# Four raw-weight slots with their own places in the load order, and an earlier copy-out, in a Strassen-like down-projection

## What is computed

```python
def swiglu(h, w_gate, w_up, w_down):
    return (jax.nn.silu(h @ w_gate) * (h @ w_up)) @ w_down
...
    yp = yp + swiglu(rms_norm(yp, g_ffn[l]), w_gate[l], w_up[l], w_down[l])
    ys = ys + swiglu(rms_norm(ys, g_ffn[l]), w_gate[l], w_up[l], w_down[l])
y_prompt = rms_norm(yp, g_final)
y_sample = rms_norm(ys, g_final)
```

## Time and profile before

| | |
|---|---|
| median of 3 runs | 1066.26 us (1065.92 to 1066.47) |
| the profiled execution, its time | 1065.66 us |
| the profiled execution, its span | 1063.9 us |
| PE busy | 1022.2 us, 96% of the span |
| DVE, ACT, POOL busy | 59%, 37%, 36% |
| mean granted clock of PE | 0.99 of full speed |

### The profile page before, as it was taken

The page is one execution under the profiler, slowest core; times in us unless marked ns, Lnnn a source line. Parts: engine busy times, 40 slices in busy tenths (PEclk is TensorE's granted clock), DMA queues, the critical chain, the costliest instruction groups (busy, mean ns, idle before and its releaser), DMA issues.

```text
span 1063.9 us, 19541 instructions
## 1 busy us (share of the span) xinstructions
PE 1022.2 (96%) x7160; PEld 934.2 (88%) x7160; DVE 625.9 (59%) x943; ACT 391.0 (37%) x763; POOL 385.3 (36%) x445
## 2 busy tenths in 40 slices
PE   5999999999999699999999999999999969999996
PEld 5999998888887599999999999999999737877785
DVE  5376547665444766666676576567665554454524
ACT  5412144444232433333333333333334354424331
POOL 2010100000000437676686596686762300120045
PEclk9999999999999899999999999999999989999999
DMA  8211331101222434364454544643637898777714
GB/s 282 90 39 42 81 83 43 40 1 64 95 100 90 116 97 147 109 198 133 124 173 123 159 140 125 186 144 110 188 117 261 271 359 293 240 267 254 269 40 163
DMA packets 176258, 155.84 MB, mean 146 GB/s; under 512 B 22352, under 2 KB 143760, under 8 KB 176208
## 3 DMA queue, kind: packets, MB, share of 16 engines
q1 hardware_dynamic: 176208, 155.16, 46.1%
HBM read 114.17 MB, written 41.06 MB: 146 GB/s over the span
## 4 chain that ended last, share of the span: by engine, by line
PE 88%; DVE 4%; DMA 4%; POOL 1%; issue 1%; ACT 1%; SPq 0%; POOLq 0%; ACTq 0%; DVEq 0%
PE ps L1033 27%; PE ps L1034 26%; PE ps L1035 26%; DMA xd_in<-act_scratch 2%; PE ps L1070 1%; PE ps L1364 1%; PE ps L1205 1%; PE ps L1183 1%; DMA act_scratch<-act_sums 1%; DMA out_state_gmlp_v_sample<-work 1%; PE ps L1167 1%; DVE work L1831 1%; DMA y_acc_odd<-in_w_down 1%; DVE ln_st L1825 1%; DMA gain<-in_g_mix 0%
## 5 line engine op out<-in xcount | busy, mean ns | idle before, releaser
L1033 PE MATMUL ps<-x_forms,w_forms 128*128 128x256 f32 (+1 forms) x1232 | 354.0, 287 | 10.5 <-DVE w_forms L1746 8.3
L1034 PE MATMUL ps<-x_forms,w_forms 128*128 128x256 f32 (+1 forms) x1232 | 355.0, 288 | 0.0
L1035 PE MATMUL ps<-x_forms,w_forms 128*128 128x256 f32 (+1 forms) x1232 | 353.6, 287 | 0.0
L1033 PEld LDWEIGHTS ps<-x_forms,w_forms 128*128 128x128 f32 x1232 | 236.3, 192 | 11.2 <-DVE w_forms L1746 5.8
L1035 PEld LDWEIGHTS ps<-x_forms,w_forms 128*128 128x128 f32 x1232 | 236.1, 192 | 0.0
L1034 PEld LDWEIGHTS ps<-x_forms,w_forms 128*128 128x128 f32 x1232 | 235.8, 191 | 0.0
L1033 PE MATMUL ps<-w_dn,x_dn 128*128 128x512 f32 x308 | 121.3, 394 | 0.0
L1035 PE MATMUL ps<-w_dn,x_dn 128*128 128x512 f32 x308 | 119.9, 389 | 0.0
L1034 PE MATMUL ps<-w_dn,x_dn 128*128 128x512 f32 x308 | 119.9, 389 | 0.0
L1746 DVE TENSOR_TENSOR w_forms<-w_sums,w_forms 128x512 fp32r<-128x512 f32 x88 | 74.1, 843 | 68.1 <-ACT w_forms L1570 67.7
L885 POOL TENSOR_SCALAR meansq<-sumsq 128x1 f32<-128x1 f32 (+1 forms) x27 | 10.4, 386 | 256.3 <-ACT xn_ffn L1410 227.0
(11 more groups left out here) (234 smaller groups left out, 2071.2 us busy)
## 6 DMA issues: line engine op xcount, KB each, us to landing
xd_in<-act_scratch SPq DMA_DIRECT2D x35, 512.0 KB, 7.1
t_raw<-in_w_down SPq DMA_DIRECT2D x88, 128.0 KB, 2.6
act_scratch<-act_sums SPq DMA_DIRECT2D x22, 512.0 KB, 4.0
y_acc_odd<-in_w_down SPq DMA_DIRECT2D x22, 512.0 KB, 5.6
wd_in<-t_scratch SPq DMA_DIRECT2D x20, 512.0 KB, 7.1
wd_in<-in_w_down SPq DMA_DIRECT2D x15, 512.0 KB, 6.2
stage<-in_w_in SPq DMA_DIRECT2D x28, 256.0 KB, 3.6
w_stage_even<-in_w_gate SPq DMA_DIRECT2D x22, 256.0 KB, 3.4
```

Of the source, the lines that this page charges most:

```text
L1033: mm(out, wh, xh, start=first, stop=False, skip_group_check=onto)
L1034: mm(out, wh, xl, start=False, stop=False, skip_group_check=onto)
L1035: return mm(out, wl, xh, start=False, stop=last, skip_group_check=onto)
```

## The change

The raw loads of the sample's first half get four slots (each a whole row of `y_acc_odd`), those of the second half keep two; the places of the raw loads in SP's order are listed in a table of their own, RAW_LOADS, which names the group (n, g) before whose loads they stand; r2 and r3 go behind the loads of group 7, before `store_sums`. The turn after (1,0) is dropped and one after (1,4) added. And `copy_out(0)` stands on ScalarE behind the forming of two groups of stage 1 (k = 6 and 7), not six.

```diff
-SAMPLE_TURNS = {(0, 3): 2, (0, 5): 2, (1, 0): 2, (1, 1): 2, (1, 2): 2, (1, 3): 1,
+SAMPLE_TURNS = {(0, 3): 2, (0, 5): 2, (1, 1): 2, (1, 2): 2, (1, 3): 2, (1, 4): 1,
                 (3, 0): 2, (3, 2): 2, (3, 4): 2, (4, 0): 2, (4, 2): 2, (4, 3): 1}
-RAW_SLOTS = 2
+EARLY_SLOTS, LATE_SLOTS = 4, 2
+
+RAW_LOADS = {(1, 2): range(4, 6), (1, 5): range(6, 8), (2, 2): range(8, 10), (2, 4): range(10, 11),
+             (3, 5): range(11, 13), (4, 1): range(13, 15), (4, 3): range(15, 17), (5, 0): range(17, 19),
+             (5, 2): range(19, 21), (5, 4): range(21, 22)}
+
+def raw_slot(r):
+    return (r % EARLY_SLOTS, r // EARLY_SLOTS + 1) if r < CHUNKS else (
+        EARLY_SLOTS + (r - CHUNKS) % LATE_SLOTS, (r - CHUNKS) // LATE_SLOTS + 1)
...
-        raw = [y_odd[:, 2 * x:2 * x + 2, 0:512] for x in range(RAW_SLOTS)]
+        raw = [y_odd[:, x, :].rearrange("p (e c) -> p e c", e=2) for x in range(EARLY_SLOTS)]
+        raw += [y_odd[:, 2 * x:2 * x + 2, 0:512] for x in range(LATE_SLOTS)]
...
             def load_raw(r):
 
                 h, c = divmod(r, CHUNKS)
-                if r >= RAW_SLOTS:
-                    sp.wait_ge(raw_used, r - RAW_SLOTS + 1)
+                slot = raw_slot(r)[0]
+                if r < EARLY_SLOTS:
+                    sp.wait_ge(product_done, product_count(last, P4, 0))
+                elif r < CHUNKS:
+                    sp.wait_ge(raw_used, r - EARLY_SLOTS + 1)
                 else:
-                    sp.wait_ge(product_done, product_count(last, P4, 0))
+                    sp.wait_ge(raw_used, max(CHUNKS, r - LATE_SLOTS + 1))
...
-            for r in range(RAW_SLOTS):
+            for r in range(2):
                 load_raw(r)
             store_step(CHUNKS - 1, 1)
...
             for k in (GROUPS_A_FORM, GROUPS_A_FORM + 1):
                 load_w(k)
                 load_x(k)
+            for r in range(2, EARLY_SLOTS):
+                load_raw(r)
             store_sums(CHUNKS - 1)
...
                 for g in range(2 if n == 1 else 0, GROUPS_A_FORM):
-                    if g >= 2:
-                        for r in range(max(RAW_SLOTS, raws_before(n - 1, g - 2)), raws_before(n - 1, g - 1)):
-                            load_raw(r)
+                    for r in RAW_LOADS.get((n, g), ()):
+                        load_raw(r)
                     load_w(GROUPS_A_FORM * n + g)
                     load_x(GROUPS_A_FORM * n + g)
-                for r in range(raws_before(n - 1, 4), raws_before(n, 0)):
-                    load_raw(r)
...
             for n in range(STAGES - 1):
-                for g in range(GROUPS_A_FORM):
+                ahead = 2 if n == 0 else GROUPS_A_FORM
+                for g in range(ahead):
                     form_hi(n + 1, g)
                 if n in (0, 1, 3):
                     for t in range(TILES):
                         copy_out(n, t)
+                for g in range(ahead, GROUPS_A_FORM):
+                    form_hi(n + 1, g)
```

More of the change, by code:

```diff
@@ L477, in build @@
         sample_landed = [sem(f"sample_landed{x}") for x in range(2)]
-        raw_landed = [sem(f"raw_landed{x}") for x in range(RAW_SLOTS)]
+        raw_landed = [sem(f"raw_landed{x}") for x in range(EARLY_SLOTS + LATE_SLOTS)]
         raw_used = sem("raw_used")
@@ L801, in load_raw @@
                 h, c = divmod(r, CHUNKS)
-                if r >= RAW_SLOTS:
-                    sp.wait_ge(raw_used, r - RAW_SLOTS + 1)
-                else:
-                    sp.wait_ge(product_done, product_count(last, P4, 0))
-                sp.dma_start(raw[r % RAW_SLOTS], w_down[:, 2 * c:2 * c + 2, 512 * h:512 * h + 512]
-                             ).then_inc(raw_landed[r % RAW_SLOTS], 16)
+                slot = raw_slot(r)[0]
[3 more added lines that the diff above has]
+                    sp.wait_ge(raw_used, r - EARLY_SLOTS + 1)
+                else:
+                    sp.wait_ge(raw_used, max(CHUNKS, r - LATE_SLOTS + 1))
+                sp.dma_start(raw[slot], w_down[:, 2 * c:2 * c + 2, 512 * h:512 * h + 512]).then_inc(raw_landed[slot], 16)
             def load_resid(k):
@@ L1361, in down_sample @@
                     pe.wait_ge(u2_down, TILES)
-                pe.wait_ge(raw_landed[r % RAW_SLOTS], 16 * (r // RAW_SLOTS + 1))
+                slot, count = raw_slot(r)
+                pe.wait_ge(raw_landed[slot], 16 * count)
                 for e in range(2):
                     last = mm(ps[QUARTERS[(2 * c + e) % 4], SAMPLE_BANK, :], sample_in[e][:, c, :],
-                              raw[r % RAW_SLOTS][:, e, :], start=c < 2, stop=c >= CHUNKS - 2)
+                              raw[slot][:, e, :], start=c < 2, stop=c >= CHUNKS - 2)
                 last.then_inc(raw_used, 1)
```

## The result

The changed kernel took 1053.93 us (median of 4 runs, 1052.11 to 1054.63); the kernel before, beside it, 1066.37 (1065.92 to 1068.01). The ratio is 0.9878, 95% interval [0.9861, 0.9895]. On the median shown before, 1066.26, that is 1053.3 us, 13.0 less. The forecast was 1054.4 and 11.9 less, in a range from 1053.4. So the direction and nearly the whole size came out, and the time by the ratio lies 0.1 us under the range's lower end. The two medians themselves lie 12.4 us apart, which would be 1053.8: the ratio goes nearly with the means of the four executions on each side, and of those of the kernel before one, at 1068.01, stands 1.5 us above the next.

A forecast was written before the change was run, and what follows sets the result against it. From 819 us on, TensorE's own matmuls plus one 9.1 us wait for a raw w_down load bound the kernel. Terms -9.16 - 2.08 - 0.75 + 0.1 = -11.9 us, from 1066.26, gave 1054.4 us; range 1053.4 to 1058.8.

The forecast's parts named there:

- The stall of 9.16 and its 2.08 of slow clock: Down-projection, turn r2,r3 before group (1,0): TensorE's 9.16 us wait and 2.08 us of lower clock go, -11.24 us.
- Turn r4,r5, -0.75: Down-projection, stage 1: this turn moves behind group (1,1) and finds its data, -0.75 us.
- The copy as a second wall: ScalarE's copy_out(0) also holds group (1,0), until about 859.7 us with r2 early alone; moved earlier, no stall.
- The stores slip by 2.7 us: r2 and r3 before the stores of the sums move SP's resumption from 845.2 to 848.0 us.
- w8 landed 14.6 us after r0: Load w8 in SP's queue, ahead of group 8's forming: lands at 855.8 us, with r0 at 841.22.
- 1.36 us a unit: Full load queue, as from 850 to 870 us: each 512 KB transfer takes 1.36 us at 385 GB/s.
- 0.1 us at tile 3 of (2,0): Stage 2: add_sample(0) done at 890.6 us, tile 3 begins at 890.58; 0.1 us of stall taken.
- Rival B: Queue binds at 335 GB/s: 4.5 us of new stall at tile 3 of (2,0), then 1058.9 us; chance 0.22.
- Second half, cost 0 with 0.7 us of margin: Sample's second half: raw loads moved earlier still let copy_out(3) begin in time, margin 0.7 us, cost 0.
- part 4: Prediction's step on the second half's loads: copy_out(3) may begin up to 961.4 us, TensorE wanting tile 0 at 962.07.
- The sum: Whole kernel: -9.16 - 2.08 - 0.75 + 0.1 = -11.9 us, against 1066.26 us gives 1054.4 us.
- under it lies only more than the 12 us there are: Whole kernel's time: claim that the range can end at 1053.4 us, as only 12 us are there to gain.

The follow-up runs named there:

- trace 1: First profiled execution of the changed kernel, no further edit; median in that measurement 1053.93 us, stretch from r0 to the last matmul 202.06 us.
- traces 2 and 3: Profiles of the changed kernel, no edit, timed again beside follow-up kernels: 1054.30 us (ratio 0.9889) and 1054.19 us (0.9892); stretch from r0 203.6 us in both.

## Why the prediction was right or wrong, point by point

- **The stall of 9.16 and its 2.08 of slow clock**: right. (1,0) began 10.38 us after r0 (850.07 - 839.69), foretold 851.59 - 841.22 = 10.37.
- **Turn r4,r5, -0.75**: right, 0.99 us in the trace after.
- **The copy as a second wall**: right, and shown from both sides; the slots alone made the kernel 4.6 us slower. The copy began within 0.1 us of where it was expected, on the scale of r0.
- **The stores slip by 2.7 us**: a size off, on both sides. Counted from r0, SP came out 1.8 us later than before in trace 1 and 3.2 and 3.4 in traces 2 and 3 (7.2 and 7.4 us after r0, against 4.0 before).
- **w8 landed 14.6 us after r0**: right in traces 2 and 3 (14.8 and 14.6), 1.7 us too late for trace 1 (12.9). The step from SP's exit to w8 was reckoned 0.2 to 0.8 us too long.
- **1.36 us a unit**: right for the queue's rate (385 GB/s before, 389 in trace 1) and for each landing but one. The prediction named landings further apart than 1.36 us between 852 and 886 as a sign that it is wrong, and that sign is there: w13 or x12 comes 1.2 to 1.5 us late in all three traces, 0.4 with the second half's loads put back, and no run shows why. The Trainium skill's figure for HBM transfers ("DMA: Bandwidth & Descriptors", "Where 436 GB/s comes from", about 358 GB/s) is not what bounded this core in these runs.
- **0.1 us at tile 3 of (2,0)**: the place was right, the size was that of an edge: nothing in trace 1, 1.1 us in traces 2 and 3. That trace 1 came out so near was luck, since the early w8 and the late w13 cancelled. Rival B was not a rival but a part of what happens, at a quarter of the price that I gave it, and by one late landing and the stores, not by a lower rate.
- **Second half, cost 0 with 0.7 us of margin**: the cost is right. The margin was 1.2 us: the copy began 1.87 us ahead of (4,0), where by part 4 it may begin 0.67 ahead (962.07 - 961.4).
- **The sum**: 11.9 foretold; the stretch from r0 gives 12.0 in trace 1 and 10.5 in the other two, against a single stretch of before; the ratios give 13.0, 11.8 and 11.5. What makes up the 1.0 to 1.3 us between the two measures is not shown; it is no more than r0 moves by from one execution to the next.
- **The step that failed** is the lower end of the range, "under it lies only more than the 12 us there are". It took all that lies ahead of the change for fixed, a term put at nothing. It is not: the changed kernel in trace 1 was 1.53 us ahead before r0, and single executions of one kernel lie 1 to 5 us apart (before: 1063.12 to 1068.27 over all chips here, 1064.50 to 1068.27 on one). With three executions of before to go by, which happened to lie within 0.6 us, a lower bound 1 us from the forecast was too narrow; the mechanism needed no wider one. By how little it was missed is chance as well: 13.0 us by the ratio is outside, the 12.4 between the medians is inside, and both later measurements, 1054.4 and 1054.7 on 1066.26, are too.

## What to carry to other kernels

When a wait is to be removed, ask what else is queued to end at the same moment: here a load and a copy both ended within a few microseconds, on different queues, and each alone was worth nothing or less. Then write down, for the transfers that follow, the landing time of each by one rate and the time when each is wanted; the smallest difference is what is left of the gain, and one trace may not show that it is small: here two errors of over 1 us each cancelled in the first. Easing one needer left the next in the same queue as tight as it was; with more slots and the queue in the order of need the waits of all of them were gone.

## What was not expected of the hardware

The landing of the last 512 KB store to `act_scratch`, told by when SP goes on, varied by 1.6 us between executions of one kernel (5.8 to 7.4 us after r0), though the queue's rate from 850 to 870 did not (383 to 389 GB/s in the three). In a run of landings about 1.36 us apart one came 1.2 to 1.5 us late in each of these traces, at the same rate of the queue; the cause is open. In the idle of 17 us the granted clock was 0.58 from 855 to 865, as in the idle of before, and the two groups behind it took 12.6 us instead of 10.8.
